# Router by token tiles with four heads at a time, rows by index begun inside it, and 88 up units beside it

## What is computed

```python
q = (xb @ w_q).reshape(T, 8, 2, 128)                   # 8 heads, 2 halves
s = jnp.einsum('thpd,hpkd->thpk', q, sub_keys)         # 128 keys for each half
sv, si = lax.top_k(s, 16)
cand = sv[:, :, 0, :, None] + sv[:, :, 1, None, :]     # 16 x 16 sums
top_s, pos = lax.top_k(cand, 16)                       # over the 256
eidx = take(si[...,0]*128 + si[...,1], pos)            # one of 16384 experts
gate = jax.nn.softmax(top_s)
act = jax.nn.gelu(einsum('thkd,td->thk', expert_u[eidx], xb))
out = einsum('thk,thkd->td', gate * act, expert_v[eidx])
```

## Time and profile before

| | |
|---|---|
| time, median of 3 runs | 2709.02 us (2704.39 to 2715.56) |
| the profiled execution | 2700.42 us, span 2699.1 us |
| TensorE (PE) busy | 2418.8 us, 90% |
| VectorE (DVE) busy | 1926.1 us, 71% |
| ScalarE (ACT) busy | 1002.4 us, 37% |
| GpSimd (POOL) busy | 760.2 us, 28% |
| mean granted clock of TensorE | 0.97 of full speed |

### The profile page before, as it was taken

One profiled execution on the slowest core, in us unless ns is written; L12 is line 12 of the kernel. 1 busy time (PEld: TensorE's weight loads), 2 busy tenths in 40 slices (PEclk: granted clock), 3 DMA queues, 4 the chain that ended last, 5 costly groups with the idle time before them and its releaser, 6 DMA issues.

```text
span 2699.1 us, 33461 instructions
## 1 busy us (share of the span) xinstructions
PE 2418.8 (90%) x12402; PEld 2007.4 (74%) x12402; DVE 1926.1 (71%) x3519; ACT 1002.4 (37%) x1686; POOL 760.2 (28%) x512
## 2 busy tenths in 40 slices
PE   7989988988888898989899899799877889999997
PEld 5768988988888887989888887588544577545555
DVE  7899889886777777988989996643467645155554
ACT  3332333333333332323333334422356524244443
POOL 4010444440111125767777771200000020000001
PEclk9999999999999998989999999899899999999999
DMA  6446444445777679999999993111000012100001
GB/s 239 178 166 248 140 137 140 138 142 204 251 256 251 245 270 367 374 342 346 364 367 357 365 358 129 55 60 58 32 1 1 17 55 78 57 23 13 18 1 63
DMA packets 162225, 465.93 MB, mean 173 GB/s; under 512 B 15504, under 2 KB 72976, under 8 KB 159632
## 3 DMA queue, kind: packets, MB, share of 16 engines
q1 hardware_dynamic: 100368, 304.40, 31.5%
q0 software_dynamic: 36864, 134.23, 13.6%
q10 hardware_dynamic: 24832, 25.17, 2.9%
HBM read 411.31 MB, written 52.43 MB: 172 GB/s over the span
## 4 chain that ended last, share of the span: by engine, by line
PE 57%; DVE 23%; DMA 8%; issue 7%; ACT 4%; POOL 1%; DVEq 0%; ACTq 0%
PE psum L412 5%; PE psum L413 5%; PE psum L414 5%; PE psum L420 5%; PE psum L422 4%; PE psum L421 4%; DVE weights_low L1347 4%; PE psum L524 4%; DMA arena<-in_v_rows,arena 3%; DMA arena<-in_u_rows,arena 2%; DVE arena L1544 2%; PE psum L836 2%; PE psum L438 2%; DVE arena L1530 2%; DMA arena<-hidden 2%
## 5 line engine op out<-in xcount | busy, mean ns | idle before, releaser
L1347 DVE TENSOR_TENSOR weights_low<-arena,weights_high 128x1024 fp32r<-128x1024 f32 x290 | 401.6, 1385 | 273.5 <-ACT weights_high L913 271.4
L913 ACT ACTIVATE weights_high<-arena 128x1024 fp32r<-128x1024 f32 x355 | 374.6, 1055 | 425.8 <-PE psum L553 285.5
L551 PE MATMUL psum<-hidden_high,weights_high 128*128 128x384 f32 x1024 | 353.5, 345 | 58.5 <-DVE hidden_low L1574 51.2
L420 PE MATMUL psum<-x_high,weights_high 128*128 128x384 f32 x1024 | 357.8, 349 | 36.3 <-POOL weights_low L1861 29.4
L421 PE MATMUL psum<-x_low,weights_high 128*128 128x384 f32 x1024 | 349.1, 341 | 0.0
L422 PE MATMUL psum<-x_high,weights_low 128*128 128x384 f32 x1024 | 349.0, 341 | 0.0
L553 PE MATMUL psum<-hidden_high,weights_low 128*128 128x384 f32 x1024 | 347.5, 339 | 0.0
L552 PE MATMUL psum<-hidden_low,weights_high 128*128 128x384 f32 x1024 | 347.2, 339 | 0.0
L412 PE MATMUL psum<-x_high,weights_high 128*128 128x512 f32 (+1 forms) x696 | 277.4, 399 | 25.3 <-DVE weights_low L1347 20.4
L413 PE MATMUL psum<-x_low,weights_high 128*128 128x512 f32 (+1 forms) x696 | 272.3, 391 | 0.0
L414 PE MATMUL psum<-x_high,weights_low 128*128 128x512 f32 (+1 forms) x696 | 272.1, 391 | 0.0
(11 more groups left out here) (237 smaller groups left out, 4295.5 us busy)
## 6 DMA issues: line engine op xcount, KB each, us to landing
arena<-in_stream SPq DMA_DIRECT2D x227, 512.0 KB
arena<-in_v_rows SPq DMA_DIRECT2D x128, 512.0 KB
arena<-in_ada_w SPq DMA_DIRECT2D x48, 512.0 KB, 3.3
hidden<-arena SPq DMA_DIRECT2D x128, 192.0 KB, 3.5
router<-arena SPq DMA_DIRECT2D x12, 2048.0 KB
arena<-hidden SPq DMA_DIRECT2D x128, 192.0 KB
arena<-router ACTq DMA_DIRECT2D x16, 1536.0 KB
arena<-in_pair_w SPq DMA_DIRECT2D x8, 576.0 KB, 3.7
```

Of the source, the lines that this page charges most:

```text
L420: PE.matmul(bank[b][:, 0:N], wh[u % 2][:, k, :], xh[:, k, PICKED:T], start=k == 0, stop=False)
L551: PE.matmul(out, wh[w][:, n, :], hh[:, r, :], start=e == 0, stop=False)
L913: ACT.activation(wh[u % 2], slots[u % RING], AF.Copy).then_inc(*tick("weights_high", u))
L1347: DVE.tensor_tensor(wl[u % 2], slots[u % RING], wh[u % 2].bitcast(F32), ALU.subtract).then_inc(*tick("weights", u))
```

## The change

- *Jobs for heads.* The router is done in eight jobs: job j is tile j // 2 of the tokens with four heads (0 to 3, or 4 to 7). A job is the same amount of work as a head before. The `qf` copies are gone, TensorE reads q itself; scores alternate between two pairs of banks (0, 1 and 2, 3), so that the keys of job j + 1 are issued two units after job j's first unit; there are two `ex` tiles, and a job's softmax is finished (`finish_gates`) inside the next job. ScalarE's Exp of a job stands at the first unit of the next.
- *Units.* JOB_UNIT gives the unit at which a job's share of up units begins: 0, 8, 17, 29, 41, 53, 65, 77, 88. So 88 up units stand beside the router (their weights_low on GpSimd) and 39 beside the scatter, 32 of them with three quads each. There VectorE makes the one-hots ahead of the next unit's weights_low.
- *Rows.* The first tile's indices are known after job 1, and the rows begin there: GpSimd fetches the first four between units 18 and 21, and jobs 2 to 7 use 6, 10, 10, 10, 10 and 10 rows, each put between two dependent steps of VectorE's router work (`rest`). In the scatter stage there is one row in every second unit, and two in each of the last eight: 32. Down units take the rest, `(left + units left - 1) // units left` at each. ROW_LAG grows from 12 to 62.
- Only the three tiles of the dense tokens are transposed for the scatter.

```diff
-UNDER_HEAD = 8
-UNDER_ROUTER = HEADS * UNDER_HEAD
+JOBS = 2 * NT
+JOB_UNIT = [0, 8, 17, 29, 41, 53, 65, 77, 88]
+UNDER_ROUTER = JOB_UNIT[-1]
-ROW_LAG = 12
+JOB_ROWS = [0, 0, 6, 10, 10, 10, 10, 10]
+ROW_LAG = sum(JOB_ROWS) + 6
...
+    for step in ROW_STEPS:
+        kind, n = step
+        if kind == "job":
+            more = JOB_ROWS[n]
+        elif kind == "up":
+            more = n % 2 if n < KEYS - UNDER_ROUTER - LAST_UPS else 2
+        else:
+            more = (len(ROWS) - used + LAST_ROWS - n - 1) // (LAST_ROWS - n) if n < LAST_ROWS else 0
+        ROWS_AT[step] = list(range(used, used + more))
+        used += more
+    FETCH_AT = {}
+    for j in range(JOBS):
+        for k, row in enumerate(ROWS_AT["job", j]):
+            n = JOB_UNIT[j] + (k + 1) * (JOB_UNIT[j + 1] - JOB_UNIT[j]) // JOB_ROWS[j] + 1
+            FETCH_AT.setdefault(min(n, UNDER_ROUTER), []).append(row)
...
# TensorE
+        def keys_of(job):
+            t, heads = job // 2, range(job % 2 * 4, job % 2 * 4 + 4)
+            for i in range(2):
...
+                elif job >= 2:
+                    PE.wait_ge(*at("found", (job - 2, i)))
+                for n, head in enumerate(heads):
+                    last = PE.matmul(bank[job % 2 * 2 + i][:, n * KEYS:(n + 1) * KEYS],
+                                     q[:, head * 2 + i, t * P:(t + 1) * P], sub_keys[:, head * 2 + i, :], start=True, stop=True)
+                last.then_inc(*tick("keyed", (job, i)))
+        for n in range(UNDER_ROUTER):
+            up_unit(n)
+            if n == 0:
+                keys_of(0)
+            if n - 2 in JOB_UNIT[:JOBS - 1]:
+                keys_of(JOB_UNIT.index(n - 2) + 1)
...
# ScalarE
+        for n in range(UNDER_ROUTER):
+            if n in JOB_UNIT[1:]:
+                job = JOB_UNIT.index(n)
+                exponents_of(job - 1)
+            up_unit(n)
+            if n in JOB_UNIT[1:]:
+                gelu_rows(("job", job))
...
# VectorE, inside route(job)
+            def rest(key, inst, at_least=0):
+                inst.then_inc(*tick("step", key))
+                if len(rows_left) > at_least:
+                    use_row(rows_left.pop(0))
+                DVE.wait_ge(*at("step", key))
...
-            step(("cand", head), last)
+            rest(("cand", job), last, 8)
...
# VectorE, scatter stage
         for n in range(1, KEYS - UNDER_ROUTER):
-            low_weights(unit("up", UNDER_ROUTER + n) + 1)
             for i in range(quads_before(n - 1), quads_before(n)):
                 one_hots(i)
+            low_weights(unit("up", UNDER_ROUTER + n) + 1)
             for j in ROWS_AT["up", n]:
                 use_row(j)
...
# GpSimd
+        for i in range(UNDER_ROUTER + 1):
+            u = unit("up", i) + 1
+            POOL.wait_ge(*at("weights_high", u))
+            POOL.tensor_tensor(wl[u % 2], slots[u % RING], wh[u % 2].bitcast(F32), ALU.subtract).then_inc(
+                *tick("weights_pool", u))
+            if i == JOB_UNIT[2] + 1:
+                POOL.wait_ge(*at("chosen", 0))
+            if JOB_UNIT[2] + 1 <= i < JOB_UNIT[2] + 1 + ROW_RING:
+                fetch_row(i - JOB_UNIT[2] - 1)
+            for row in FETCH_AT.get(i, []):
+                fetch_row(row + ROW_RING)
```

More of the change, by code:

```diff
@@ L186, in write @@
     gate = area(84, NT, ENTRIES)
-    qf = [area(24, T), area(25, T)]
     scr = area(26, 2, NT, KEYS)
@@ L218, in write @@
     rows = [area(first, D) for first in (14, 72, 74, 80)]
-    choice_f, chosen, row_act, row_w = (columns_at(85 * T + i * P, P) for i in range(4))
+    choice_f, chosen, row_act, row_w = (columns_at(91 * T + i * P, P) for i in range(4))
     row_acc = area(86, D)
@@ L342, in write @@
         ROWS += [("u", n)] * (n < ENTRIES) + [("v", n - ROW_LAG)] * (n >= ROW_LAG)
-    ROW_STEPS = [("up", n) for n in range(1, KEYS - UNDER_ROUTER)] + [("down", e) for e in range(KEYS)]
+    ROW_STEPS = [("job", j) for j in range(JOBS)] + [("up", n) for n in range(1, KEYS - UNDER_ROUTER)] + [
+        ("down", e) for e in range(KEYS)]
     ROWS_AT = {step: [] for step in ROW_STEPS}
     LAST_ROWS = KEYS - 4
[L346 to L351, removed]
+    used = 0
+    for step in ROW_STEPS:
[13 more added lines that the diff above has]
+            FETCH_AT.setdefault(min(n, UNDER_ROUTER), []).append(row)
     GELU_AT = {}
@@ L497, in up_unit @@
             on_rest(unit("up", i), 4 + i % 4)
-        for head in range(HEADS):
-            up_unit(head * UNDER_HEAD)
+        def keys_of(job):
+            t, heads = job // 2, range(job % 2 * 4, job % 2 * 4 + 4)
             for i in range(2):
-                PE.wait_ge(*at("qf", (head, 1)))
-                if head == 0 and i == 0:
+                if job == 0 and i == 0:
                     PE.wait_ge(*at("q_a", 14))
                     PE.wait_ge(*at("q_v", 15))
[L506 to L513, removed]
+                elif job >= 2:
[10 more added lines that the diff above has]
+                keys_of(JOB_UNIT.index(n - 2) + 1)
         def scatter(i):
@@ L1016, in scalar, with exponents_of, gelu_rows @@
                 *tick("x_rows", half))
[L1017 to L1027, removed]
+        def exponents_of(job):
+            ACT.wait_ge(*at("lowered", job))
+            ACT.activation(ex[job % 2], ex[job % 2], AF.Exp).then_inc(*tick("ex", job))
+        def gelu_rows(step):
+            for g in GELU_AT.get(step, []):
+                part = row_act[:, g * GROUP:(g + 1) * GROUP]
+                ACT.wait_ge(*at("row_used", ROWS.index(("u", (g + 1) * GROUP - 1))))
+                ACT.activation(part, part, AF.Gelu_apprx_tanh).then_inc(*tick("row_act", g))
+        for n in range(UNDER_ROUTER):
[5 more added lines that the diff above has]
+                gelu_rows(("job", job))
         def stage_gates(i):
@@ L1042, in load_gates @@
                               *tick(f"g{block % 2}_in", block, 16))
[L1044 to L1048, removed]
+        exponents_of(JOBS - 1)
         up_unit(UNDER_ROUTER)
@@ L1462, in vector @@
                     last = DVE.match_replace(scr[:, i, t, :], val[:, i, t, 0:8], score[i][:, t, :], -3e38)
-            step(("scr", head), last)
+            rest(("scr", job), last, 10)
             for i in range(2):
@@ L1467, in vector @@
                     last = DVE.max_index(ind[:, i, t, 0:8].bitcast(U32), val[:, i, t, 0:8], score[i][:, t, :])
-                last.then_inc(*tick("found", (head, i)))
-            DVE.wait_ge(*at("found", (head, 1)))
+                last.then_inc(*tick("found", (job, i)))
+            if len(rows_left) > 9:
+                use_row(rows_left.pop(0))
+            DVE.wait_ge(*at("found", (job, 1)))
+            if job:
+                finish_gates(job - 1)
             for i in range(2):
@@ L1481, in vector @@
                 last = DVE.max(top[:, t, 0:8], cand[:, t, :])
-            step(("top", head), last)
+            rest(("top", job), last, 7)
             for t in range(NT):
                 last = DVE.match_replace(scr2[:, t, :], top[:, t, 0:8], cand[:, t, :], -3e38)
-            step(("scr2", head), last)
+            rest(("scr2", job), last, 6)
             for t in range(NT):
@@ L1501, in vector @@
                 place = abf[:, i, :, :].rearrange("p t (k o) -> p (t k) o", o=1).to_broadcast([P, NT * TOPK, TOPK])
-                step(("eq", head, i), DVE.tensor_tensor(eq, iota16, place, ALU.is_equal))
+                step(("eq", job, i), DVE.tensor_tensor(eq, iota16, place, ALU.is_equal))
                 for t in range(NT):
@@ L1506, in vector @@
                         e, e, indf[:, i, t, :].rearrange("p (o a) -> p o a", o=1).to_broadcast([P, TOPK, TOPK]), ALU.mult)
[L1507 to L1521, removed]
+                rest(("picked", job, i), last, 1 - i)
+                step(("idx", job, i), DVE.tensor_reduce(
+                    idx[i][:, tile, cols].rearrange("p (n k) -> p n k", k=TOPK),
+                    eq.rearrange("p (t k) a -> p t k a", t=NT), AX.X, ALU.add))
         def use_row(j):
@@ L1545, in use_row @@
                     *tick("row_used", j))
+        for job in range(JOBS):
+            route(job)
+            if job == 1:
+                step("choice", DVE.scalar_tensor_tensor(choice_f, idx[0][:, 0, :], float(KEYS), idx[1][:, 0, :],
+                                                        ALU.mult, ALU.add))
+                DVE.tensor_copy(chosen.bitcast(U32), choice_f).then_inc(*tick("chosen", 0))
+        finish_gates(JOBS - 1)
         keys = iota.rearrange("p (o k) -> p o k", o=1).to_broadcast([P, QUAD, KEYS])
@@ L1856, in gpsimd @@
             gather("ffn", c)
[L1858 to L1862, removed]
         def fetch_row(j):
@@ L1879, in weigh_hidden @@
             POOL.tensor_tensor(one, one, gates, ALU.mult).then_inc(*tick("weighted", e))
[L1881 to L1884, removed]
+        for kind, n in ROW_STEPS[JOBS:]:
             if kind == "down":
```

46 lines of the change are left out of this document (30 added, 16 removed).

## The result

The changed kernel takes 2610.6 us (median of 4 runs, 2610.1 to 2622.6), the kernel before 2706.7 (4 runs, 2704.0 to 2715.6): a ratio of 0.965, interval 0.961 to 0.969. The forecast was 2678, range 2648 to 2714. So the direction was right, and the gain was three times as large as forecast: 96 us instead of 31 (2709 less 2678). The profiled execution has a span of 2608.8 us, 90.3 less than before.

What follows compares the result with a forecast made beforehand. TensorE, paced by GpSimd, was taken to bound the router (end 689.4 us), TensorE the scatter, DMA and VectorE the old downs; -13 us up to the downs and -18 in them, -31 against 2709.0, gave 2678, range 2648 to 2714.

Steps and rivals of the forecast that it cites:

- The scatter stage: Scatter beside 39 up units: TensorE 9.0 us per three-quad unit, VectorE 6.7 and hidden; 333.8 us, downs start 13 us earlier.
- All four rivals: VectorE rows waiting for GpSimd 11%, downs giving nothing back 14%, lower TensorE clock in the scatter 6%, all going well 10%.
- The clock rival: Scatter: half of the 32 three-quad units followed by a lower-clock stretch of 1.6 us, losing 26 us: 2704 us; 6%.
- The router: Router beside 88 up units: TensorE, paced by GpSimd, ends unit 88 at 689.4 us.
- The stall per job: Router, TensorE: falls from 3.63 to 1.93 us as ScalarE's Exp wait of 1.70 goes and the table load stays.
- The lower clock: Router, TensorE behind each stall: the 1.6 us it costs go; if it stays, 13 us.
- The rows' cost to TensorE: Router: 0.15 us of waiting for GpSimd in each of the 71 units from job 2 on, 11 us.
- a sign of being wrong: Router: GpSimd waiting for rows, or VectorE's row instructions averaging over 2.8 us, would show the prediction wrong.
- r = 2.1: Router, VectorE: us per row including waits for GpSimd's subtraction; 56 rows cost 118 us, so VectorE ends at 681 us.
- the port rival: Router: each VectorE row waits a full GpSimd subtraction, r = 3.7, shifting everything by 81 us: 2759 us; 11%.
- The keys' second pair of banks: Router: a job's keys are there two units into the job before, ending VectorE's 5.5 us wait per head.
- The downs: Down stage: 44 two-row units at 5.45 us, 80 one-row units at 4.22; 596 us against 614.5, -18 us.

Runs made afterwards that it cites:

- the run that undid it: The changed kernel with VectorE making weights_low ahead of the one-hots again in the scatter stage; 2678.9 us, ratio 0.992.
- Even rows: The changed kernel with the downs' 168 rows spread evenly over 124 units, run twice; 2598.3 us (ratio 0.961) and 2597.2 us (0.962).

## Why the prediction was wrong, step by step

- **The scatter stage: the step that failed.** "VectorE per unit: 1.2 + 3 x 1.63 + 0.65 = 6.7 us, TensorE 4.07 + 4.9 = 9.0, so VectorE stays hidden, and one-hots first changes nothing that is waited for." VectorE's 6.7 was right (216.45 us in 32 units). TensorE's 9.0 was not its own work but the length of a loop that held three waits for VectorE's one-hots; its own work is 4.24 + 3 x 0.87 = 6.84. TensorE's 1.63 per quad and VectorE's 1.63 per quad stood in the earlier trace rows, and I used both in one sentence without asking why they were equal. What led away from it was the profile's "issue" behind half a microsecond of idleness. The Trainium skill (Perfetto Trace Analysis, section Per-instruction lifecycle: what the profiler-reported window actually captures) says that the time an instruction waits for semaphores is outside its recorded slice. The rows agree: the wait for the one-hots shows only as a gap of 0.41 to 0.50 us in front of the matmuls. Size: 66.3 us, and 67.3 in the run that undid it.
- **No rival named it.** All four rivals and the forecast took 1.63 us per quad as given. The clock rival looked at the same stage and did not come: the granted clock is 1.00 in the 222 us with three quads a unit.
- **The router: the end is right, 688.1 for 689.4, its terms only in part.** The stall per job was put at 1.93 us beyond the pace and is 1.70 at the one above (1.53 + 0.34 - 0.17). The lower clock went, as argued from the 2.01 us in the earlier trace rows. The rows' cost to TensorE was put at 11 and is 10.0, but by another way than the forecast's. GpSimd's subtraction grew from 2.51 us on average without rows to 2.58 with them, not by 0.15. And GpSimd waited for rows six times, 11.1 us in all, which the prediction had named as a sign of being wrong. That the two ways give nearly the same sum is luck.
- **VectorE's side of the router was too cheap.** The row cost was put at r = 2.1, which had VectorE ready at 681, 8 us ahead of TensorE. The row instructions themselves stay under that:

```profile
L1565 DVE SCALAR_TENSOR_TENSOR arena<-arena 128x1024 f32<-128x1024 f32 x56 | 94.1, 1681 | 11.2 <-DMA arena<-in_u_rows,arena 11.2
```

  (94.1 + 11.2)/56 is 1.88 us with the waits for the fetches, and 0.08 for reading the accumulator make 1.96. But the other work of VectorE got longer beside them, too: the comparison with iota, L1548, takes 2.08 us on average, 1.60 in the run without router rows, 1.23 before. All in all VectorE is busy 399.59 us with the rows and 275.78 without, so a row costs (399.59 - 275.78 + 11.2)/56 = 2.41 us. That is more than the 2.25 from which the port rival was to decide, and less than the 2.8 from which it was to lose. VectorE's last instruction of the router ends at 689.7, 1.6 us behind TensorE's unit 88 (less 135 for the rows that is 555, where the prediction's sum had 563). The rival had the mechanism right and its size (3.7) too high.
- **The keys' second pair of banks: right, and worth little.** VectorE's wait for keys fell from 43.6 to 5.3 us, but the later Exp alone brings it to 9.3 in the old kernel. What the second pair is worth in the changed one no run shows.
- **The downs: -18 forecast, -6.0 measured.** Two-row units took 5.53 us (243.2/44; I had 5.45), the others 365.3/84 = 4.35 (I had 4.22). Most of the miss is the second: 84 x 0.13 = 11 us. TensorE stood there 11 times for VectorE's hidden_low, 11.5 us in all; why so often stays open. That unevenness costs was in the sum (-18, where time by bytes would give -34), and the two comparisons show 15 to 17 us for it. Even rows give -19 to -21, so time did not quite follow the bytes.

## What to carry to other kernels

When two engines show the same interval per piece of work, look whether one of them is waiting for the other: take a stage's cost per engine from its instructions back to back, not from start to start across a gap, before calling one of them the bound. In a queue in order, a statement that waits on a long loop must not stand ahead of one that the busiest engine wants next. And when work moves between stages, keep each unit's mix of transfers and matmuls level: here that was 16 us.

## What the runs showed that I had not expected

- A quad of four 128x128 float32 matmuls takes 0.87 us when nothing is waited for (three quads, 24 recorded parts, in 2.60 us), about half of what the starts before suggested.
- In the old kernel the Exp of each head, moved two units later and nothing else, gave 28 us of router. By the prediction's estimate (8 x 1.6 us) nearly half of it was the stretch at the lower clock behind a 3.5 us stall; the clock did rise from 0.95 to 1.00.
- ScalarE's table load took 1.28 us, and the Exp began 0.02 us behind it (307.10 + 1.28, 308.40).
